# Values as the stationary operand in a batched attention, page numbers clamped once, a state copy moved

## The reference, cut to what matters

```
q, gates, nsa_rows, win_rows, q_sb, sb_rows = project(rms_norm(x), ...)
o_cmp  = softmax(q kc^T / 8 where the block has ended) vc    # kc, vc: compress() of 32-row blocks, stride 16
o_slc  = softmax(q k^T / 8 over selected 64-row blocks) v
o_win  = softmax(q k^T / 8 over the last 512) v
z      = q_sb k_sb^T / 8                                     # strictly causal
o_sb   = exp(log_sigmoid(z) + sum of log_sigmoid(-z) over later keys) v_sb
o_nsa  = gate0 * o_cmp + gate1 * o_slc + gate2 * o_win
h = x + concat(rms_norm(o_nsa), rms_norm(o_sb)) w_out ;  y = h + swiglu(rms_norm(h))
```

## Time and profile before

| | us |
|---|---|
| median of three runs | 3020.37 |
| profiled execution | 3020.68 |
| its span, first to last instruction | 3018.6 |
| PE busy (share of the span) | 2675.0 (89%) |
| DVE busy | 1256.2 (42%) |
| POOL busy | 831.3 (28%) |
| ACT busy | 798.2 (26%) |
| DMA | 314.28 MB, 104 GB/s over the span |

### The profile page before, as it was taken

The page is one execution under the profiler, slowest core; times in us unless marked ns, Lnnn a source line. Parts: engine busy times, 40 slices in busy tenths (PEclk is TensorE's granted clock), DMA queues, the critical chain, the costliest instruction groups (busy, mean ns, idle before and its releaser), DMA issues. The chain is left out here.

```text
span 3018.6 us, 45708 instructions
## 1 busy us (share of the span) xinstructions
PE 2675.0 (89%) x13736; PEld 2003.8 (66%) x13736; DVE 1256.2 (42%) x2483; ACT 798.2 (26%) x1487; POOL 831.3 (28%) x845
## 2 busy tenths in 40 slices
PE   7989699983999999999999994357989999999999
PEld 6778677772765554555555551133469999999999
DVE  3463233332656566555566650223321111114553
ACT  4232133321333333332233330001121111113332
POOL 0120244403545545454455440412200000000000
PEclk9999789995569787776688797678999999999999
DMA  4224654408245545444465346313121111113200
GB/s 143 93 88 138 159 135 129 126 21 172 85 116 157 144 127 161 135 138 122 129 162 157 119 125 219 71 43 119 57 78 47 47 45 48 46 35 111 67 29 24
DMA packets 269781, 314.28 MB, mean 104 GB/s; under 512 B 62465, under 2 KB 177986, under 8 KB 269354
## 3 DMA queue, kind: packets, MB, share of 16 engines
q1 hardware_dynamic: 238842, 266.46, 30.3%
q0 software_dynamic: 14528, 38.32, 5.1%
q10 hardware_dynamic: 16192, 6.93, 0.9%
HBM read 278.89 MB, written 37.44 MB: 105 GB/s over the span
## 5 line engine op out<-in xcount | busy, mean ns | idle before, releaser
L1070 POOL TENSOR_TENSOR late<-late 128x512 f32<-128x512 f32 x256 | 336.7, 1318 | 280.3 <-DMA late<-in_cache_sb_kv 246.5
L1995 PE MATMUL pg<-h_turned_hi,w_gu_hi 128*128 128x344 f32 x1056 | 338.5, 321 | 10.2 <-DVE h_turned_lo L2043 10.2
L1997 PE MATMUL pg<-h_turned_hi,w_gu_lo 128*128 128x344 f32 x1056 | 338.4, 320 | 0.0
L1996 PE MATMUL pg<-h_turned_lo,w_gu_hi 128*128 128x344 f32 x1056 | 338.2, 320 | 0.0
L1190 PE MATMUL decode_ps<-late,weights_dec 128*8 128x512 f32 x512 | 312.6, 714 | 9.2 <-DMA late<-in_cache_sb_kv 8.0
L1241 ACT ACTIVATE probs<-scores,minus_max 128x63 f32<-128x63 f32 (+4 forms) x192 | 109.6, 571 | 604.2 <-DVE minus_max L1314 574.4
L2121 PE MATMUL py<-w_down_hi,act_hi 128*128 128x256 f32 x792 | 225.7, 285 | 9.8 <-DVE w_down_lo L2168 9.8
L2038 DVE TENSOR_TENSOR w_gu_lo<-late,w_gu_hi 128x512 fp32r<-128x512 f32 x88 | 61.0, 693 | 401.9 <-ACT w_gu_hi L2008 401.9
L2122 PE MATMUL py<-w_down_lo,act_hi 128*128 128x256 f32 x792 | 225.0, 284 | 0.0
L2123 PE MATMUL py<-w_down_hi,act_lo 128*128 128x256 f32 x792 | 225.0, 284 | 0.0
L2104 POOL DMA_DIRECT2D out_y_prompt<-y_rows x32 | 17.4, 545 | 744.5 <-DVE y_rows L2156 744.5
(11 more groups left out here) (281 smaller groups left out, 5360.0 us busy)
## 6 DMA issues: line engine op xcount, KB each, us to landing
late<-in_cache_sb_kv SPq DMA_DIRECT2D x512, 256.0 KB, 2.9
late<-in_w_gate_up SPq DMA_DIRECT2D x88, 256.0 KB, 2.9
late<-in_cache_nsa_kv SPq DMA_DIRECT2D x160, 128.0 KB, 3.8
late<-in_cache_nsa_kv POOLq DMA_DIRECT2D x96, 128.0 KB, 3.3
late<-in_w_down SPq DMA_DIRECT2D x4, 2816.0 KB, 10.9
w_in_raw<-in_w_in SPq DMA_DIRECT2D x40, 256.0 KB, 4.8
x_sb<-in_x_prompt SPq DMA_DIRECT2D x8, 512.0 KB, 3.9
out_sb_p<-proj_sb SPq DMA_DIRECT2D x16, 256.0 KB
```

The costliest lines, as they stand in the source:

```text
L1070: eng.tensor_tensor(prod[:, p % NPR], kr[:, p % RING], qb[:, u], ALU.mult).then_inc(multiplied, 1)
L1995: eng.matmul(pg[:, e, c, 0:CW], w_hi[:, h, j, :], hT_hi[:, k, cols], start=k == 0, stop=False)
L1996: eng.matmul(pg[:, e, c, 0:CW], w_hi[:, h, j, :], hT_lo[:, k, cols], start=False, stop=False)
L1997: mm = eng.matmul(pg[:, e, c, 0:CW], w_lo[:, h, j, :], hT_hi[:, k, cols], start=False, stop=k == KT - 1)
```

## The change

- `attend` is unrolled (no hardware loop), over pairs of heads N = 0 to 3 and within them over blocks of two tiles of both heads. A block is 16 steps in the order of `BLOCK`. Queries are loaded per block and pair of heads, by POOL; values of `sb` are loaded by POOL, no longer by SP.
- PV: the values (128 keys x 64) are stationary, and the turned weights of both heads (256 columns; `sb`: one head, 128) stream. The output is transposed: 64 partitions per product. `sel` goes to partitions 0 to 63 and `win` to 64 to 127; `sb` and `cmp` use the halves for two heads or two tiles. 80 batches (5 per block) replace 256 single products; their pieces are placed in fixed steps (`PV_AT`). ACT copies the result out (`copy_out`), PE turns it back (`turn_back`), DVE scales it (`finish`).
- The sums of the weights come from ACT's exp (`accum_out`); DVE makes the factors (reciprocal times gate) when the PV pieces start (`factors`).
- Turned groups: every third on DVE, the others on ACT.
- Value pages of the samples: rings of 8; four pages in a row go to four quarters of the output partitions, with 32 stationary columns (24 of zeros). The samples' 288 steps are spread over all steps by a cost per step (`DEC`), the last sample's values included. `om` and its sum take 128 partitions.
- SP loads eight page numbers at once, unchecked.
- `compress`: DVE clamps the page table once (to float, clamp, to integer); SP and POOL wait for that. `decode_nsa`: DVE clamps the block numbers; no range checks.
- The copy of the window state moves from `decode_nsa` to `attend`'s SP queue, behind key page 16 of sample 0; the window state's loads on ACT move behind the exp of the compressed scores.

```diff
-                        if kind == "cmp":
-                            l, r = prT[0:NCP, m % 2, 0, :], vcp[0:NCP, bass.ds(kv, 1), :]...
-                        else:
-                            l, r = prT[:, m % 2, c, :], vx[:, 0 if kind == "sel" else 1, lo + c, bass.ds(kv, 1), :]...
-                        mm = eng.matmul(O[:, 0:HD if kind == "sb" else HD + 1], l, r, start=c == 0, stop=c == tiles - 1)
+                    if piece == 0:
+                        by_v, by_a = saves(groups_ready(bt))
+                        eng.wait_ge(saved[0], by_v)
+                        eng.wait_ge(saved[1], by_a)
+                        if bt:
+                            eng.wait_ge(ot_saved, bt)
+                    ...
+                    for c in range((t + 1) * piece // pieces, (t + 1) * (piece + 1) // pieces):
+                        for z in range(2):
+                            if c >= count[z]:
+                                continue
+                            if kind == "sb":
+                                l, r = vs[:, z, c, :], prT[:, SB_SLOT + c, z * P:z * P + P]
+                            else:
+                                name = ("sel", "win")[z]
+                                l, r = vx[:, z, first_tile(name, t) + c, kv, :], prT[:, slot_of(name, t) + c, :]
+                            mm = eng.matmul(O[HD * z:HD * z + HD, 0:W], l, r, start=c == 0, stop=c == count[z] - 1)
...
+                def turn_back(bt):
+                    N, t, kind, W = batch(bt)
+                    eng.wait_ge(ot_saved, bt + 1)
+                    bank_free(("out", bt))
+                    for u in range(W // P):
+                        mm = eng.transpose(PT[:, bank_of["out", bt], u * P:(u + 1) * P], oT[:, bt % 2, u * P:(u + 1) * P], ident[:, :])
...
-                            eng.matmul(DB[0:NH, :], aw[:, :, NPAGE - 1 - p], vr[:, p % RING], start=p == 0, stop=p == NPAGE - 1).then_inc(v_used, 1)
+                        for i, p in enumerate(pages):
+                            eng.matmul(DB[32 * i:32 * i + 32, :], aw[:, :, NPAGE - 1 - p], value_slot(p), start=p < SIDE, stop=p >= NPAGE - SIDE).then_inc(v_used, 1)
...
+                def copy_out(bt):
+                    N, t, kind, W = batch(bt)
+                    eng.wait_ge(pv_done, bt + 1)
+                    if bt >= 2:
+                        eng.wait_ge(out_turned, bt - 1)
+                    eng.activation(oT[:, bt % 2, 0:W], O[:, 0:W], ACT.Copy).then_inc(ot_saved, 1)
...
+        PV_AT, OUT_AT = ((8,), (10, 11), (12, 13, 14), (18, 19), (20, 21, 22)), (9, 12, 15, 20, 23)
...
+                            if p == 16 and h == 0:
+                                eng.dma_start(io["win_s_out"][:, 0:WINDOW - 1, :], io["state"][:, 1:WINDOW, :]).then_inc(row_stored_w, 16)
+                                eng.dma_start(io["win_s_out"][:, WINDOW - 1, :], io["win_new"]).then_inc(row_stored_w, 16)
...
+                eng.wait_ge(table_ready, 16)
+                eng.tensor_copy(ptf[:, :], pt[:, :])
+                eng.drain()
+                eng.tensor_scalar(ptf[:, :], ptf[:, :], 0.0, float(NPOOL - 1), ALU.max, ALU.min)
+                eng.drain()
+                eng.tensor_copy(pt[:, :], ptf[:, :]).then_inc(table_set, 1)
```

More of the change, by code:

```diff
@@ L58 @@
 TOK = SEQ + NB
+CLAMPED = "the numbers were clamped to the pool on VectorE before they are read"
 def constants():
@@ L90, in constants @@
     tri = (i >= j).astype(np.float32)
-    diag = np.zeros((NH, NH, HD), np.float32)
-    for h in range(NH):
-        diag[h, h] = 1
+    diag = np.tile(np.eye(32, NH, dtype=np.float32), (4, 1))
     return {
@@ L974, in attend @@
-        zero = lambda N: isinstance(N, int) and N == 0
-        def turns(eng, body, tail):
-            body(0, 0)
-            with eng.Fori(1, 3) as i:
-                body(i, i - 1)
-            body(3, 1)
-            for s in range(H):
-                tail(s)
+        for m in range(U):
+            N, u, t, kind = STEPS[front_of(m)]
+            G0.append(G0[-1] + (tiles_of(kind, t) + 3) // 4)
+        saver = lambda b: 0 if b % 3 == 2 else 1
+        saves = lambda b: (b // 3, b - b // 3)
@@ new lines, in attend @@
+        PT_USES = []
+        for i in range(END):
+            PT_USES += [("out", bt) for bt, _ in at_iteration(i, OUT_AT)]
+            if 2 <= i < U + 2:
+                PT_USES += [("group", b) for b in range(G0[i - 2], G0[i - 1])]
+        bank_of = {use: n % 2 for n, use in enumerate(PT_USES)}
+        use_before = {use: PT_USES[n - 2] for n, use in enumerate(PT_USES) if n >= 2}
+        cost = [0.9 + 0.4 * tiles_of(kind, t) for N, u, t, kind in STEPS]
+        DEC = [[] for _ in range(END)]
@@ L985, in attend @@
+        for n in range((NH + 1) * NPAGE):
+            goal, i, total = (n + 0.5) / ((NH + 1) * NPAGE) * sum(cost), 0, cost[0]
+            while total < goal:
+                i += 1
+                total += cost[i]
+            DEC[i].append((n // NPAGE, n % NPAGE))
+        VGROUP = {6: 0, 9: 1, 13: 2, 16: 3, 20: 4, 23: 5, 27: 6, 31: 7}
+        reduced_at = lambda s: [] if s == 0 else [s - 1] if s < NPAGE - 1 else [s - 1, s]
         with nc.Block() as block:
@@ L1192, in body @@
-                def body(N, kv):
-                    for s in range(U):
-                        scores(N, kv, s)
-                        kvb = lambda m: kv if m >= 0 else (1 if isinstance(N, int) else 0)
-                        if not (zero(N) and s < 2):
-                            transposes(N, s - 2)
-                        if not (zero(N) and s < 3):
-                            product(N, kvb(s - 3), s - 3)
-                        sample(N * 2 + s // H, s % H)
-                def tail(s):
-                    if s < 2:
-                        transposes(4, s - 2)
-                    if s < 3:
-                        product(4, 1, s - 3)
-                    sample(NH, s)
@@ new lines, in _ @@
+                for i in range(END):
+                    if i < U:
+                        scores(i)
+                    for bt, _ in at_iteration(i, OUT_AT):
+                        turn_back(bt)
+                    if 2 <= i < U + 2:
+                        transposes(i - 2)
+                    for bt, piece in at_iteration(i, PV_AT):
+                        product(bt, piece)
+                    for h, s in DEC[i]:
+                        sample(h, s)
+                sample(NH + 1, 1)
```

649 lines of the change are left out of this document (352 added, 297 removed).

## The result

The changed kernel takes 2836.09 us (median of 4 runs, 2827.81 to 2849.01) beside 3008.68 us of the kernel before on the same chip: ratio 0.9423, 95% interval 0.9372 to 0.9473. It is faster, by 173 us where 373 were forecast. The profiled execution took 2838.32 us, its span is 2836.7.

A forecast was written before the change was run, and what follows sets the result against it. PE was taken to end last in attend. Attend 300 us less, its start 10, tail 38 and decode_nsa 25 made 373 less than 3020.68: 2648 us, with a range of 2510 to 2840 at 0.80.

The forecast's parts named there:

- PE's sum: In attend, PE's full-clock work falls from 785 to 562 us with overlapping products, or rises to 841 without overlap.
- Rivals 4 and 5: In attend: tiling changes stop PE, 2797 us in total (chance 0.04); halves and quarters do not overlap, 3025 us (0.06).
- I keep 0.75 and the 3% of waiting: In attend, PE's mean clock and waiting share stay as before: 562 / 0.75 x 1.033 = 774 us.
- The stick chain: In attend, the stick-breaking rounds through ACT, DVE and POOL take 570 to 690 us over 64 rounds, covered by PE.
- Rival 3: In attend, the clock falls to 0.62 or 0.55 as PE waits more: 2803 to 2923 us in total; chance 0.14.
- a clock under 0.65: In attend, the sign that would mean Rival 3 had come.
- Rival 2: In attend, the clock rises above 0.85, the stick chain ends last: attend 620 to 690, total 2487 to 2557 us; chance 0.14.
- PE under 80% busy: In attend, the sign that the stick chain or POOL had taken over from PE.
- The other engines' sums: In attend, POOL 583 us, DVE at most 650 and ACT 515; none reaches PE's 774.
- Turn back: In attend, PE's wait for ACT's copy before turning results back costs nothing, covered by scores; uncovered 32 us.
- Small parts: Outside attend's main work: start 10 us less, tail 38 less, decode_nsa 25 less; moved state copy adds 6 to attend.
- The page numbers in compress: In compress, the clamp's three small DVE steps, about 1 us, are hidden behind the prompt's own tile; uncovered 1.5 us.

## Why the prediction was right in kind and half wrong in size

- **PE's sum: right.** 564 us of full-clock work for 562. The sum started from 785, by the mean clock of the stage; split by level the stage before has 777, so the agreement to 2 us is partly luck. The overlap that was read from the earlier trace rows holds for halves of 64 and for quads of 512 columns. Rivals 4 and 5 fall with it.
- **"I keep 0.75 and the 3% of waiting": this step failed.** It was 0.67 and 13%: busy 855.5 instead of 749 us, waits 131.6 instead of 25 (and 6 for the state copy), which makes attend 207 us longer than forecast. The step divided PE's work by a clock as if PE went on ending last. But the clock of this stage is no constant that work is divided by: it was 0.61 with 494 us of work, 0.67 with 564, 0.79 with 658 and 0.82 with 752, in 959, 987, 987 and 1037 us. Without a change of PE's products the stage went from 987 to 922 us by ACT's order and to 860 by a shorter chain: the others' round holds PE.
- **"The stick chain: 570 to 690 us. Covered now by PE": the mis-sized term behind it.** The sum added the durations of the chain's instructions and two of their neighbours. It left out that DVE, in program order, stands still ahead of the scan until ACT has made the step's exp, copied its groups and taken the logarithm, and that the next maxima, and with them ACT's exps and PE's scores, stand behind the scan. The 64 rounds took 987 us, 15.4 each, where 570 to 690 means 8.9 to 10.8. Taking DVE's wait away by ACT's order alone gave 65 us, cutting the chain to 128 columns 127; the rest of the gap to 690 was not taken apart. The trace of before showed the same wait, 65.7 us, and it was not in the argument:

```profile
DVE late L1328 <- ACT late L1256: 65.7, 57, 2.0
```

- **Rival 3 (the clock falls) came out with the time it gave**, 2836 against 2803 to 2923, but not by its sum: it had a clock of 0.62 or less with 3% of waiting, and 0.67 with 13% came. Its sign, a clock under 0.65, did not. As the whole cause it does not stand: at a level of 0.90 the stage still took 946.5 us. As a part it is not excluded: fillers that raised the level and filled waits gave 31 us there, and 45 behind the changed orders. No run changed the level alone.
- **Rival 2 (the stick chain ends last) named the place** but priced it at 620 to 690 and tied it to a rising clock. **"PE under 80% busy" as its sign was wrong:** PE was 87% busy, two thirds of that at the lower level, and the stage still got shorter with its products untouched. Work at full clock over the stage's length, 564 / 987 = 57%, would have shown the slack.
- **The other engines' sums: right as bounds.** POOL 578.8 us for 583, DVE 581.9 for at most 650, ACT 410.2 for 515. Each is far under the stage's length, so their busy time alone does not show who holds it.
- **Turn back, priced at 0 (uncovered 32):** 43.5 us at the copy and 36.3 behind it for the bank, but moving both away gained nothing.
- **Small parts: right.** Start -9.8 for -10; tail -40.2 for -38; state copy about 9 us of PE for 6. In decode_nsa the exp comes right behind the maximum, as these rows of the timeline show (compare), 14.3 us from the stage's start instead of 25.8: 11.4 us for 11.5. The rest, 20.7, was about 14 in the forecast; the stage's 32.1 lie at the end of its range (10 to 32).

```profile
1712.42 0.69 DVE L1730 TENSOR_REDUCE nmx_cmp<-SD 128x2 f32<-128x510 f32 x1 [0.78 <-PE SD L1640]
...
1713.14 0.47 ACT L1611 ACTIVATE late<-SD,nmx_cmp 128x255 f32<-128x255 f32 x1 [16.98 <-DVE nmx_cmp L1730]
1713.15 0.39 ACTq L1614 DMA_DIRECT2D kv_win<-in_state_nsa_window  x1
```

- **The page numbers in compress: 0 forecast, -6.8 measured.** The clock between 350 and 400 us was 0.62 there instead of 0.50. Whether that is the reason was not tried.

The overlap that the Trainium skill gives ("TensorE: Matmul & The Clock Gate", Part 3: Packing small matmuls: 3.07 for four row tiles, 2.38 for three column tiles) lies under what this trace has for quads, 3.8 / 1.12 = 3.4. The quads are four column tiles, for which the Trainium skill's table there has no row. The Trainium skill's page "TensorEngine Tiling (Array Packing)" (Tiling Modes, Key Properties) says that a change of tiling mode drains the engine. In the rows above no time for that shows: the scores begin 0.06 us ahead of the quad's modelled end.

What stays open: of the 207 us, the two orders, the moved copy and the fillers gave back 120. How much of the miss belongs to the round and how much to the level was not separated. What holds the round at 867 us with the wait for the logarithm gone and the clock at 0.93 was not taken apart, nor why 70 us less of PE's work gives 28 while 95 more cost none.

## What to carry to other kernels

When a change takes work from the engine that ends last, sum the next engine's round with its waits in program order, not the durations of its instructions: a wait that costs nothing today (65.7 us on DVE here) can be on the path tomorrow. A matrix engine that is 87% busy at a lowered clock can have slack; ask how much of the stage its work would fill at the full clock, and add work to see whether the time moves. That test alone does not decide, since the level can rise with the work (0.67 to 0.79 here); a change of a partner's order that leaves the matrix engine's products alone decides more. So look in the partners' lists for an instruction that waits in front of others which have their inputs already, and move that.

## What the runs showed of the hardware that was not expected

- Adding 512 products whose results nobody reads did not lengthen the stage (987.1 and 987.0 us); the granted clock went from 0.67 to 0.79, and PE's busy time from 855.5 to 844.0 us. With quicker partners 1024 of them shortened it by some 45 us (911.6 to 866.6).
- Each of the 32 falls of the clock in attend of the changed kernel came in a wait of PE or within 2.5 us behind one, most of them of 0.5 to 4 us; the low level then stayed for 3.4 to 54.6 us, in which PE was mostly busy.
- Four float32 products on quarters, 512 columns each, ran in 1.12 us for eight records at the high level and 1.96 at the low.
